# Seven-product jobs: product 4 of the job in front moved behind its product 3, with VectorE's and ScalarE's orders rewritten to match

## The reference

```python
def half_swiglu(x, g, w_gu, w_down):
    h = rmsnorm(x, g) @ w_gu                  # 1024 -> 2 * 2816
    a, b = jnp.split(h, 2, axis=-1)
    return x + 0.5 * ((jax.nn.silu(a) * b) @ w_down)
...
for i in range(DEPTH):                        # DEPTH = 2
    hp = half_swiglu(hp, norm_ffn_a[i], w_ffn_a_gu[i], w_ffn_a_down[i])
    ...                                       # retention, then stick-breaking attention
    hp = half_swiglu(hp, norm_ffn_b[i], w_ffn_b_gu[i], w_ffn_b_down[i])
    hp = ple_add(hp, p_prompt[i], norm_ple[i], ple_w_gate[i], ple_w_proj[i])
```

## Time and profile before

| what | us |
|---|---|
| median of 3 runs | 2784.4 (2784.36 to 2786.01) |
| the profiled execution | 2784.26 |
| its span in the trace | 2782.7 |
| TensorE busy in it | 2744.7 (99%) |
| VectorE busy | 1920.1 (69%) |
| ScalarE busy | 1207.2 (43%) |
| TensorE's mean granted clock | 0.996 |

### The profile page before, as it was taken

One profiled execution on the slowest core, in us unless ns is written; L12 is line 12 of the kernel. 1 busy time (PEld: TensorE's weight loads), 2 busy tenths in 40 slices (PEclk: granted clock), 3 DMA queues, 4 the chain that ended last, 5 costly groups with the idle time before them and its releaser, 6 DMA issues.

```text
span 2782.7 us, 47474 instructions
## 1 busy us (share of the span) xinstructions
PE 2744.7 (99%) x18946; PEld 2699.7 (97%) x18946; DVE 1920.1 (69%) x2691; ACT 1207.2 (43%) x1629; POOL 191.7 (7%) x190
## 2 busy tenths in 40 slices
PE   8999999999999999999999999999999999999997
PEld 8999999999999999999999999999999999999997
DVE  7888864646464678888557788865555568888755
ACT  5445443323132444454444455444534443545443
POOL 0000003101010110000010000002000020000021
PEclk9999999999999999999999999999999999999998
DMA  3322323333232313323321222223222112232231
GB/s 120 95 84 79 97 79 124 110 103 114 92 110 95 104 55 94 87 81 92 93 76 60 85 85 87 88 84 121 88 83 91 68 61 72 77 101 77 86 99 53
DMA packets 80909, 246.96 MB, mean 89 GB/s; under 512 B 8465, under 2 KB 25121, under 8 KB 79681
## 3 DMA queue, kind: packets, MB, share of 16 engines
q1 hardware_dynamic: 71408, 204.67, 23.6%
q0 software_dynamic: 9296, 39.40, 3.9%
HBM read 226.74 MB, written 17.30 MB: 88 GB/s over the span
## 4 chain that ended last, share of the span: by engine, by line
PE 97%; DVE 2%; ACT 0%; issue 0%; DMA 0%; ACTq 0%; SPq 0%; DVEq 0%
PE ps L618 42%; PE ps L547 35%; PE ps L930 7%; PE ps L806 4%; PE ps L983 2%; PE ps L599 1%; PE ps L904 1%; PE ps L1017 1%; PE ps L967 1%; PE ps L871 1%; PE ps L855 0%; PE ps L1003 0%; PE ps L874 0%; PE ps L849 0%; PE ps L883 0%
## 5 line engine op out<-in xcount | busy, mean ns | idle before, releaser
L1086 ACT ACTIVATE w_hi<-raw 128x1024 fp32r<-128x1024 f32 (+2 forms) x210 | 201.3, 959 | 522.4 <-PE ps L547 382.3
L1729 DVE TENSOR_TENSOR w_lo<-raw,w_hi 128x1024 fp32r<-128x1024 f32 (+2 forms) x210 | 238.1, 1134 | 100.5 <-ACT w_hi L1086 97.5
L547 PE MATMUL ps<-x_hi,w_hi 128*128 128x320 f32 x1216 | 283.7, 315 | 9.7 <-DVE x_lo L1734 8.7
L547 PE MATMUL ps<-x_hi,w_lo 128*128 128x320 f32 x1216 | 277.6, 310 | 0.0
L547 PE MATMUL ps<-x_lo,w_hi 128*128 128x320 f32 x1216 | 277.4, 309 | 0.0
L547 PEld LDWEIGHTS ps<-x_hi,w_hi 128*128 128x128 f32 x1216 | 204.3, 188 | 13.5 <-DVE w_lo L2472 8.7
L547 PEld LDWEIGHTS ps<-x_lo,w_hi 128*128 128x128 f32 x1216 | 203.9, 188 | 0.0
L547 PEld LDWEIGHTS ps<-x_hi,w_lo 128*128 128x128 f32 x1216 | 203.7, 188 | 0.0
L1150 ACT ACTIVATE wx_hi<-raw 128x1024 fp32r<-128x1024 f32 (+1 forms) x92 | 92.4, 1004 | 252.4 <-PE ps L618 215.1
L618 PE MATMUL ps<-x_hi,w_hi 128*128 128x320 f32 x576 | 178.7, 310 | 0.0
L618 PE MATMUL ps<-x_hi,w_lo 128*128 128x320 f32 x576 | 177.9, 309 | 0.0
(11 more groups left out here) (310 smaller groups left out, 7714.4 us busy)
## 6 DMA issues: line engine op xcount, KB each, us to landing
raw<-wst SPq DMA_DIRECT2D x292, 512.0 KB, 3.6
raw<-wst SPq DMA_DIRECT2D x96, 384.0 KB, 3.2
raw<-wst SPq DMA_DIRECT2D x32, 256.0 KB, 2.6
s<-st_d POOLq DMA_DIRECT2D x8, 1024.0 KB, 5.1
sts_o<-s POOLq DMA_DIRECT2D x16, 512.0 KB, 3.3
rd<-dec_d POOLq DMA_DIRECT2D x8, 640.0 KB, 5.5
kc<-kc_d POOLq DMA_DIRECT2D x8, 512.0 KB, 4.3
vc<-vc_d POOLq DMA_DIRECT2D x8, 512.0 KB, 5.2
```

Of the source, the lines that this page charges most:

```text
L547: last = nc.tensor.matmul(out[:, h, :], a, b[:, HALF * h:HALF * (h + 1)], start=start and q == 0, stop=stop and q == 2, skip_group_check=True)
L1086: nc.scalar.activation(w_hi[:, (c["n"] + m) % 2, 0:cols], raw[:, r, 0:cols], ACT.Copy).then_inc(s_whi, 1)
L1729: tt(w_lo[:, p, 0:cols], raw[:, r, 0:cols], w_hi[:, p, 0:cols].bitcast(F), ALU.subtract).then_inc(s_wlo, 1)
```

## The change

TensorE: in a job that has a job in front, product 4 of that one now follows directly on its product 3, ahead of the job's own products 2 and 6. VectorE: `c12` moves ahead of `s3`, `gated` and `g_sum` ahead of `lo12` and `s4`; behind a dn job `c21` moves ahead of all sums and low parts for the next job. ScalarE: `silu(made)`, `hi34(d)` and `ghi(made)` now stand ahead of `hi12(new)` and `snap2(d)`. The first job of piece 1 and the first dn job of a piece keep their orders. No instruction is added or taken away. Lines behind the edit on ScalarE have numbers 3 lower than in the kernel before, VectorE's among them.

```diff
@@ TensorE, winograd
                             third(old)
-                            second().then_inc(s_prod[2], 1)
-                            sixth().then_inc(s_prod[6], 1)
                             if after_start:
                                 split_up_to("T4")
                             fourth(old)
+                            second().then_inc(s_prod[2], 1)
+                            sixth().then_inc(s_prod[6], 1)
                             fifth()
@@ ScalarE, winograd
                             hi1(new)
                             snap2(d)
                             hi2(new)
-                        elif new:
-                            hi12(new)
-                        if made and made["seven"]:
+                        if made:
                             silu(made)
-                            snap2(d)
-                        elif old:
-                            snap2(d)
-                            if made:
-                                silu(made)
                         hi34(d)
                         if made:
                             ghi(made)
+                        if old:
+                            if new:
+                                hi12(new)
+                            snap2(d)
                         if d["kind"] == "gu":
                             snap3(d)
@@ VectorE, winograd
                         if summed:
                             c11_c12(summed)
-                            s1_s2(new)
-                            s3(new)
                             c21(summed)
-                            lo12(new)
-                            s4(new)
+                            if new:
+                                s1_s2(new)
+                                s3(new)
+                                lo12(new)
+                                s4(new)
                             lo34(d)
                             continue
                         if new:
                             s1_s2(new)
+                        if made:
+                            c12(made)
+                        if new:
                             s3(new)
+                        if made:
+                            gated(made, 1)
+                            if made["seven"] and made["odd"]:
+                                g_sum(made, 1)
+                            gated(made, 0)
+                            if made["seven"]:
+                                g_sum(made, 2)
+                        if new:
                             if old:
                                 lo12(new)
                             else:
                                 lo1(new)
                                 lo2(new)
-                        if made:
-                            c12(made)
-                            gated(made, 1)
-                            if made["seven"] and made["odd"]:
-                                g_sum(made, 1)
-                        if new and made and made["seven"]:
-                            s4(new)
-                        if made:
-                            gated(made, 0)
-                            if made["seven"]:
-                                g_sum(made, 2)
-                        if new and not (made and made["seven"]):
                             s4(new)
                         lo34(d)
```

## The result

| kernel | us, median | against before, 95% |
|---|---|---|
| before | 2784.4 | |
| changed | 2810.9 (2808.75 to 2812.76) | 1.0093 (1.0078 to 1.0108) |

The change costs 26.5 us, 0.93%. The forecast was 2808, with 2796 to 2822 around it. The profiled execution took 2812.76 us with a span of 2811.2, against 2784.26 and 2782.7.

What follows compares the result with a forecast made beforehand. TensorE, busy 99% of the span, bounds the kernel. New waits of 3.71 (piece 1), 1.27 (piece 2) and 0.90 us (first dn jobs) make 5.88 per FFN, 23.5 for four: 2808 us, 0.84% slower, range 2796 to 2822.

Steps and rivals of the forecast that it cites:

- the break at the first dn job: First dn job, first FFN: product 7 waits 0.59 us for ScalarE's snapshot; 8 such breaks, 4.7 us in all, expected to stay.
- rival 2: Kernel gains: old 4 sooner removes the 0.59 us waits in first dn jobs, 4.7 us, to 2779.6; chance 0.04.
- Old 4 and c22: Gu jobs, S being product 1's start: old 4, due S+3.53, needs c22, ending S+3.08; fits by 0.4 us.
- The links: Loop in gu jobs: load 3.8, s1_s2 to c12 1.33, c12 to hi12 3.20 or 4.41, hi12 to lo34's end 4.18 us.
- The waits: Product 7 waiting for snap2 in gu jobs: 3.71 us in piece 1, 1.27 in piece 2, none in piece 3.
- s1_s2 waiting for the load in nearly every job: Sign expected in the profile after: VectorE's s1_s2 held by the load from memory in nearly every job.
- First dn jobs: Pieces 1 and 2: VectorE enters up to 0.9 us late, glo needed mid-job; 0.45 us taken, twice per FFN.
- The other price of the load: Load from lo34 to s1_s2 priced by the skill's 3.2 us estimate instead of the trace: about 3.6 us per FFN, 2799.
- No new wait: Gu jobs: the snapshot comes in time after all and the time stays, 2782 to 2789; chance 0.08.
- a gain: Earlier old 4 lets the job in front finish sooner, removing first dn job waits: 2779.6; chance 0.04.
- old 4 waiting for VectorE: Jobs 3 and 5 of both pieces: VectorE 1 us later, old 4 waits 0.6 us, 10 us on top, 2818; chance 0.09.
- The clock: TensorE's clock falls behind the 12 longest new waits, 1.7 us each, 20 on top: 2828; chance 0.05.

Runs made afterwards that it cites:

- the half loads: Changed kernel with the gu slot loads of pieces 1 and 2 halved (512 of 1024 columns): 2793.5 us, ratio 1.0035.

## Why the prediction was right

- **What bounds the kernel.** Right: TensorE without a gap, so that nothing was to be won. The kernels with one of the two links opened, or both, came out within 0.1% of before. One number was read wrongly. I took the break at the first dn job as 0.59 us from the chain, which counts it from the snapshot's start; from start to start it is 0.32, so 2.6 us in all and not 4.7. The sum wasn't touched, since that wait stays; the most that a gain could have brought was smaller than rival 2 had it.
- **Old 4 and c22.** Right: no wait on c22 in the changed kernel. In job 3 c22 starts at S+2.60 by the working, 2.55 measured (135.41, with product 1 at 132.86), and the wait is nowhere in the list.
- **The links.** 3.20 and 4.41 us from c12 to hi12 were 3.19 and 4.40; 4.18 to lo34's end was 4.16; the load, taken as 3.8, was 3.63 in job 2. All came from rows of a kernel in which these steps stood in another order; in these rows VectorE's and ScalarE's times for an operation didn't change with its place (lo34 1.22 us, hi12 1.06 and 1.04).
- **The waits.** Predicted for piece 1: 0.72, 1.38, 0.23, 1.38; measured 0.88, 1.14, 0.20, 1.37. For piece 2: 1.27 in job 4 and nothing else; measured 1.23, and 0.12 in job 3. That the long ones behind the first fall on the jobs with an odd made was right, and so was that piece 2 loses less because it comes in with slack, and that piece 3 loses nothing. "s1_s2 waiting for the load in nearly every job" was too much: it does in jobs 1, 2 and 4, and the working itself had VectorE as the later one in job 3.
- **First dn jobs.** The size was a choice between two bounds, and the place was wrong. I had 0.45 us each for glo in mid-job; measured were 0.31 in seven of eight and 0.6 in one, at the job's very start, where product 3 of the job in front comes first and wants lo34, not 1.76 us into the job as in others.
- **The load's spread.** In the fourth FFN job 1 loses 2.07 us, the longest of all: from lo34's end to s1_s2 its load took 5.0 us (2384.36 to 2389.36). In the second FFN one of 4.49 us (1252.48 to 1256.97) goes with 0.30 us lost in job 5 of piece 2, where none was forecast. Loads vary in the kernel before too (the earlier trace rows have 3.74 and 4.34), and there VectorE's idle time took it up.
- **How 23.5 came out as 26.5.** In the profiled executions the waits in gu jobs are 22.0 us where the sum had 19.9, those of the first dn jobs 2.8 where it had 3.6. The slower starts behind the waits, 2.1 us, and the 1.6 us outside the FFNs had no term. So the nearness is in part luck: one term was too large, and the changed kernel's load in its first jobs was under the 3.8 put in (3.63 in job 2) while a few later ones were well over.
- **The other price of the load.** The Trainium skill, DMA: Bandwidth & Descriptors, section Anatomy of one DMA, gives about 2.0 us fixed and the bytes at 436 GB/s on GpSimd's path, an estimate of 3.2 us for 512 KB. By it the result would have been about 2799 (3.6 us for an FFN, of which the gu jobs are 3.1 when the working is done again). The profile of the changed kernel has a median of 3.6 from issue to landing, and s1_s2 starts 3.63 after lo34 in job 2. The trace was the better guide.
- **Rivals.** No new wait, a gain, old 4 waiting for VectorE: none came in the changed kernel. The last is what the kernel with ScalarE's order of before shows. The clock didn't fall behind the new waits either, but one comparison for it was read wrongly: in the 1.23 us of the earlier trace rows TensorE did not stand idle, its timeline has ten matmuls of L890 there (549.38 to 550.69). A longer wait than any of mine did bring the clock down in another kernel: see below. Outside the FFNs the low stretch of the earlier trace rows lasted longer in the changed kernel: a granted clock of 0.50 from 731.5 to 738.2 us, before from 725.8 to 729.0. Behind it the changed kernel is 1.0 us later. No run shows why.

## What to carry to other kernels

Before something is put behind another step in an engine's list, follow what that step waits for all the way round: here a snapshot wanted 1.8 us after its product came to hang on a load from memory, over two engines, and the loop was 0.2 to 1.4 us longer than TensorE's job in most of the jobs it held. Such a loop is found by adding its links and comparing with one period of the bounding engine. Here it could be opened at either of two links, by putting hi12 ahead of ghi again or by moving lo34 into the 2 us in which VectorE waited for hi12. Shortening a link helps only until the next slowest way round takes over, as the half loads showed. TensorE, at 99%, had nothing to give to a reordering, but idle time of the other two that hides a wait can be lost to one.

## What the runs showed of the hardware beyond that

When TensorE's order was put back, waits of 2.64 us from start to start in the midst of dense matmuls (listed as 2.33 idle) were followed by matmuls at half clock, at 0.265 us each for about 11. The longest waits of the changed kernel, up to 1.6 and once 2.2 us from start to start (2393.18 to 2395.40), were not: the window behind the latter has a granted clock of 1.00 (seventh entry).

```profile
2395.40:2398.40 3.00, 3.00 (x20) 3.00 (x21) 2.97 (x4) 1.76 (x3) 0.00 (x0) 1.00 0.00 0
```

So the loss of a wait isn't in proportion to its length: there 2.49 us of waiting cost about 3.9. Nor is a long wait the only thing that the clock fell behind. In the kernel before it went down at 2248 us too, where TensorE's last pause was one of 0.95 us and what it had done since 2244 us was mostly small matmuls (busy 3.05 of 4.00 us):

```profile
2248.10:2251.40 3.30, 3.30 (x8) 1.03 (x10) 0.58 (x2) 0.54 (x2) 0.00 (x0) 0.50 0.54 164
```

The wait of 2.2 us is a single one, and all sixteen long ones are of one schedule. What decides between them no run here settles.
